# A gate matrix in DRAM, laid out by sets of four key rows instead of by slabs of 16 tokens

## What is computed

```python
q = jnp.einsum('td,de->te', xb, w_q).reshape(tb, PEER_HEADS, 2, PEER_QDIM // 2)
s = jnp.einsum('thcd,hckd->thck', q, sub_keys).astype(jnp.float32)
sv, si = lax.top_k(s, K)
...
top_v, top_j = lax.top_k(cand, K)
eidx = jnp.take_along_axis(cidx, top_j, axis=-1)
gw = jax.nn.softmax(top_v, axis=-1)
u = exp_u[eidx]
v = exp_v[eidx]
a = jax.nn.gelu(jnp.einsum('td,thkd->thk', xb, u).astype(jnp.float32))
return jnp.einsum('thk,thkd->td', (gw * a).astype(dt), v)
```

## Time and profile before

| | us |
|---|---|
| time, median of 3 runs | 2099.42 (2092.5 to 2101.09) |
| time of the profiled execution | 2092.99 |
| its span, first to last instruction | 2091.2 |
| PE busy | 2024.9 (97%) |
| DVE busy | 942.0 (45%) |
| ACT busy | 363.8 (17%) |
| stores of the gates, issue to landing, median | 5.0 |
| loads of the gates, issue to landing, median | 15.9 |

### The profile page before, as it was taken

The page is one execution under the profiler, slowest core; times in us unless marked ns, Lnnn a source line. Parts: engine busy times, 40 slices in busy tenths (PEclk is TensorE's granted clock), DMA queues, the critical chain, the costliest instruction groups (busy, mean ns, idle before and its releaser), DMA issues.

```text
span 2091.2 us, 30654 instructions
## 1 busy us (share of the span) xinstructions
PE 2024.9 (97%) x12876; PEld 1975.2 (94%) x12876; DVE 942.0 (45%) x1506; ACT 363.8 (17%) x568; POOL 192.6 (9%) x216
## 2 busy tenths in 40 slices
PE   7999999999799999989999999999999999999996
PEld 7998998898599999989999999999999999999995
DVE  5444454575742996852333333333333333333304
ACT  4333555344332003210000000000000000000000
POOL 1000122000000000010000111111101111111000
PEclk9899999999899999999999999999999999999998
DMA  7454433755244666898888889899999898998841
GB/s 285 162 183 180 151 131 111 292 180 223 100 163 153 249 262 223 301 352 287 306 297 296 323 337 338 332 333 371 352 333 342 339 336 335 333 347 332 303 162 41
DMA packets 124066, 547.73 MB, mean 262 GB/s; under 512 B 57952, under 2 KB 58016, under 8 KB 59600
## 3 DMA queue, kind: packets, MB, share of 16 engines
q1 hardware_dynamic: 52496, 374.36, 47.7%
q0 software_dynamic: 20096, 147.04, 19.2%
q10 hardware_dynamic: 51392, 25.17, 4.6%
HBM read 530.74 MB, written 14.68 MB: 261 GB/s over the span
## 4 chain that ended last, share of the span: by engine, by line
PE 95%; DVE 2%; DMA 2%; ACT 0%; issue 0%; POOL 0%; SPq 0%; DVEq 0%; ACTq 0%
PE bank L774 32%; PE bank L793 22%; PE bank L473 16%; PE bank L488 9%; PE bank L717 9%; PE bank L737 2%; DMA gbuf<-gate_matrix 1%; DMA ring_raw<-in_stream 1%; PE bank L513 1%; DVE hres L1247 1%; PE bank L571 0%; PE bank L515 0%; DVE hres L1253 0%; PE bank L593 0%; PE bank L578 0%; PE bank L704 0%
## 5 line engine op out<-in xcount | busy, mean ns | idle before, releaser
L774 PE MATMUL bank<-wE,experts 128*128 128x192 f32 x4096 | 668.2, 326 | 0.9 <-DVE wE L1439 0.9
L774 PEld LDWEIGHTS bank<-wE,experts 128*128 128x128 f32 x4096 | 665.8, 190 | 1.5 <-issue 1.5
L793 PE MATMUL bank<-h2T,experts 128*128 128x192 f32 x2816 | 459.4, 326 | 0.0
L793 PEld LDWEIGHTS bank<-h2T,experts 128*128 128x128 f32 x2816 | 457.9, 190 | 0.0
L1070 DVE TENSOR_TENSOR ring_lo<-ring_raw,ring_hi 128x2048 fp32r<-128x2048 f32 x97 | 222.1, 2291 | 210.9 <-ACT ring_hi L817 210.6
L473 PE MATMUL bank<-actT_hi,ring_hi 128*128 128x256 f32 x912 | 263.7, 289 | 15.0 <-DVE ring_lo L1070 12.1
L473 PE MATMUL bank<-actT_lo,ring_hi 128*128 128x256 f32 x912 | 261.3, 287 | 0.0
L473 PE MATMUL bank<-actT_hi,ring_lo 128*128 128x256 f32 x912 | 261.2, 286 | 0.0
L1449 DVE TENSOR_TENSOR accT<-accT,bank 128x384 f32<-128x384 f32 x120 | 61.1, 551 | 432.0 <-PE bank L774 432.0
L717 PE MATMUL bank<-h2T,experts 128*128 128x192 f32 x1280 | 219.5, 329 | 8.0 <-ACT early L1002 8.0
L717 PEld LDWEIGHTS bank<-h2T,experts 128*128 128x128 f32 x1280 | 209.8, 192 | 8.3 <-ACT early L1002 8.3
(11 more groups left out here) (209 smaller groups left out, 1356.1 us busy)
## 6 DMA issues: line engine op xcount, KB each, us to landing
experts<-in_stream SPq DMA_DIRECT2D x256, 1024.0 KB, 7.0
ring_raw<-in_stream SPq DMA_DIRECT2D x97, 1024.0 KB, 4.8
gate_matrix<-stage ACTq DMA_DIRECT2D x12, 1024.0 KB, 5.0
gbuf<-gate_matrix ACTq DMA_DIRECT2D x32, 384.0 KB, 15.9
gb<-in_ln_g POOLq DMA_DIRECT2D x3, 1024.0 KB, 12.3
gb<-in_ln_b POOLq DMA_DIRECT2D x3, 1024.0 KB, 16.9
act_raw<-in_xT SPq DMA_DIRECT2D x4, 512.0 KB, 9.0
hres<-in_x POOLq DMA_DIRECT2D x1, 2048.0 KB, 9.3
```

The lines of the kernel that those rows point to most:

```text
L774: last = pe.matmul(outs[d // 2][:, (d % 2) * ND:(d % 2 + 1) * ND], experts[:, x % RP, c4 * 512 + d * P:c4 * 512 + (d + 1) * P], wE[:, c, : ...
L793: last = pe.matmul(bank[(N_U + c) % 2][:, 0:ND], experts[:, x % RP, ko * P:(ko + 1) * P], h2T[:, ko, :], start=(ko == 0), stop=(ko == KO - 1))
```

## The change

The DRAM tensor gets the shape (partition, set of four rows k, slab, 4 rows x 16 tokens). What one load needs is then one run of 3072 bytes in each partition (12 slabs x 64 elements), where it was 12 pieces of 256 bytes. What one store writes in a partition is then 32 pieces of 256 bytes (one for each set of four rows), where it was one run of 8192 bytes. The SBUF tiles `stage` and `gbuf` and the bytes moved stay as they were, and so do all instructions of all engines and their order; only the shapes of the 12 stores and the 32 loads differ.

```diff
-        gdram = nc.dram_tensor("gate_matrix", (P, N_STAGE, P, STAGE_T), F32, kind="Internal").ap()
+        gdram = nc.dram_tensor("gate_matrix", (P, P // 4, N_STAGE, 4 * STAGE_T), F32, kind="Internal").ap()
...
-                    act.dma_start(gdram[:, sn], stage[:, b]).then_inc(stage_out[b], 16)
+                    act.dma_start(gdram[:, :, sn, :], stage[:, b].rearrange("p (q c) t -> p q (c t)", c=4)).then_inc(stage_out[b], 16)
...
-                act.dma_start(gbuf[:, b], gdram[:, :, 8 * g + 4 * b:8 * g + 4 * b + 4, :]).then_inc(g_landed[b], 16)
+                act.dma_start(gbuf[:, b].rearrange("p s c t -> p (s c t)"),
+                              gdram[:, 2 * g + b].rearrange("p s c -> p (s c)")).then_inc(g_landed[b], 16)
```

## The result

| | before | after |
|---|---|---|
| median of 20 runs, us | 2101.06 (2091.39 to 2105.21) | 2110.49 (2100.16 to 2113.72) |
| ratio, 95% interval | | 1.0047 (1.0033 to 1.0062) |
| span of the profiled execution, us | 2091.2 | 2100.9 |

The changed kernel is 0.47% slower: some 9.9 us, and 9.7 us between the two profiled spans. That is just inside the 10.5 us taken as "same", and clear of no change by its interval, which reaches to 13 us on the other side. The executions of either kernel fall in two groups, 9 to 11 us apart, and both profiled ones (2092.99 and 2102.58) belong to the shorter group.

A forecast was written before the change was run, and what follows sets the result against it. PE, busy for 97% of the span, was taken to bound the kernel. 5.6 us for the last store and 1.5 for the stage made 7.1 us, on the median of before 2106.5, rounded 2107; range 2096 to 2141.

The forecast's parts named there:

- The place and the sign: At the first gate loads before line 774, the one hitch near the gate matrix, 12.1 us; line 774 starts 5.6 us later.
- What is removed: Gate loads in long runs free ACT, but line 774 then waits for DVE's twelfth gathered row: gain 1.2 to 4.4 us.
- The price of a piece: A 256-byte piece of a store takes 20 ns of a DMA engine, between bounds of 17.6 and 30 ns.
- The stage: From 805 to 912 us the twelve stores need 61.4 us against 60.0 free; 1.5 us lost for bursty traffic.
- The last store: Issued at 906.76, it starves beside the gathers' burst, lands near 936, and starts line 774 5.6 us later.
- The rule of one piece a turn: A DMA queue of 256-byte pieces moves one piece for each 8 KB packet of the others, some 0.6 us a turn.
- The sum: Last store 5.6 us plus stage 1.5 us: 7.1 us, giving 2106.5 on the median of before, rounded 2107.
- my own case: Stores at 18 to 22 ns a piece, the last landing near 936: 2104 to 2110 us, chance 0.47.
- Pieces of 22 ns or more: Stores fill the DMA queue and PE waits in the stage: loss 10.4 us at 22 ns, 37 at 30; chance 0.40.
- A store through before the burst: Last store through before gathers or faster in turns; ACT free by 915 to 921, gain 1.2 to 4.4 us, chance 0.13.

The follow-up runs named there:

- e3: Kernel before, with each gate load reading one run of 3072 bytes in a partition (wrong gates), stores unchanged: ratio 0.9995 to before.
- e2: Kernel before, with six gathered rows of DVE moved from ahead of line 774 into the groups behind: ratio 0.9941 to before.
- e5: Changed kernel, with GpSimd waiting for all twelve stores before it issues its ninth gather: ratio 1.0029 to before.
- e7: Changed kernel with sets of eight key rows: 512-byte pieces in stores, one load of 6144-byte runs for a group: ratio 1.0031 to before.

## Why the prediction was right

**The place and the sign.** The one hitch near the gate matrix is where the whole difference lies: 9.3 us of rest, and no difference behind the start of line 774. Right.

**What is removed.** I gave it 1.2 to 4.4 us if the stores cost nothing; e3 measured 1.8. That the gathered rows of DVE stand behind the loads was the step that mattered, and e3 shows it (8.86 us for DVE). A slip without effect: the 32 matmuls of the earlier trace rows are all of slot 39, not 16 of 0.326 us and a tail. e2's 136 matmuls in 22.27 us make 5.2 us for 32, the same length.

**The price of a piece.** 20 ns an engine taken, 18.2 measured; the bounds 17.6 and 30 held it. The lower one had been read from loads, and the upper one is the same number times the slowing within a store. The read-modify-write that the Trainium skill (DMA: Bandwidth & Descriptors, Specifications) puts on transfers below 512 bytes doesn't show as a cost of writing: 18.2 ns for a piece of a store, 17.6 for one of a load.

**The stage.** The sum gave 61.4 us against 60.0 free. Measured, the stores took 0.499 x 107 = 53.4 us, and the other two queues left 0.521 x 107 = 55.7: the piece was cheaper than in the sum, but the other queues took more, which the sum had held fixed. The share is 0.98, with PE uninterrupted. I had added 1.5 us for bursts and none was lost. ACT's waits of 9.9 us and a median landing of 11.2 us (8 to 10 expected) were covered by the four PSUM banks.

**The last store.** Expected at about 936, measured at 940.1. This is the term that was too small, in two places. I let 155 pieces an engine through before the burst, and it was 103. Part of that is the room: I took 3.1 us for it without saying from where (the row leaves 0.606 x 6 = 3.6), and the changed kernel's q10 had 41.7% of 6 us, 2.5 us, 360 packets of the store before among them. And I gave the remainder 1.5 us from 933 on, as if the queues then stayed empty: most of it did go in a gap, but another gather took 90.1% of the engines from 936 to 940. The rule of one piece a turn was right: 405 pieces beside 406 and 379 packets. By the Trainium skill's 9 to 17 descriptors a turn (same page, Queues, rings and completion order) the 100 pieces of the prediction would have been through by 921; this trace doesn't bear that out for pieces that a store writes, nor did for a load's.

**The sum.** 5.6 us for the last store and 1.5 for the stage made 7.1; it was 9.3 (by the rest) and 0. The two errors partly cancel, which is luck. Against the median of 20 runs of before, 2101.06, the 7.1 us make 2108, and 2110.49 was measured, 0.5 us above the 2104 to 2110 that I had given my own case.

**The rivals.** Pieces of 22 ns or more: no. A store through before the burst: no, but e5 shows what it would have done for ACT, and also what it costs to bring it about by holding the gathers back.

## What to carry to other kernels

Moving small pieces from reads to writes isn't neutral even if the bytes and the pieces are the same: look at which of the two everything waits for, and what shares the engines with it at that moment. A transfer in small pieces beside two queues of large packets gets one piece a turn, so price the last such transfer by the pieces that are left when the others start, and not by its mean time; e7 suggests that even a few count. And where PE stands at a hand-over, first ask what could be moved out of that stretch: moving six gathers, with DVE's work on them, was worth 12.3 us by the rest (0.59% by the runs), more than the 9.3 us between the layouts.

## What the runs showed of the hardware that I hadn't expected

- A 512-byte piece of a store takes some 30 ns of an engine (e7, 906 to 910) against 18.2 ns for one of 256 bytes, so doubling the piece saves less than a quarter of a store's engine time (128 x 30 = 3.8 us against 4.7).
- One piece beside one packet holds with engines half idle too: 27 and 27 at 55% (changed kernel, 911 to 912).
- A store with about 5% of its packets left at 914 (e7) lands nearly as late after its issue as one with 60% left at 913 (changed kernel): 28.5 us against 33.0.
- The issue of a store in pieces takes ACT 0.52 us, where one in long runs took 0.33, and 1.2 to 2.2 us in four of twelve cases; what sets these apart wasn't isolated.
